# The order of wide and narrow products inside the FFN parts of a two-block transformer kernel

## What is computed

```python
def swiglu(x, w_gate, w_up, w_down):
    return (jax.nn.silu(x @ w_gate) * (x @ w_up)) @ w_down

h = h + 0.5 * swiglu(rms_norm(h, ffn1_norm[l]), ffn1_w_gate[l], ffn1_w_up[l], ffn1_w_down[l])   # FFNs 0 to 3
...
gu = h @ w_ffn_gu                                                                               # FFNs 4 and 5
ffn = (jax.nn.silu(gu[..., :D_FF_2]) * gu[..., D_FF_2:]) @ w_ffn_down
return x + rms_norm_2(ffn, n_post_ffn)
```

## Time and profile before

| | |
|---|---|
| median of 3 runs | 1903.11 us |
| the profiled execution's own time | 1903.32 us |
| its span | 1901.2 us |
| TensorE busy | 99% of the span |
| VectorE busy | 70% |
| ScalarE busy | 51% |
| GpSimd busy | 8% |
| DMA | 327.28 MB, 172 GB/s mean |

### The profile page before, as it was taken

The page is one execution under the profiler, slowest core; times in us unless marked ns, Lnnn a source line. Parts: engine busy times, 40 slices in busy tenths (PEclk is TensorE's granted clock), DMA queues, the critical chain, the costliest instruction groups (busy, mean ns, idle before and its releaser), DMA issues.

```text
span 1901.2 us, 26155 instructions
## 1 busy us (share of the span) xinstructions
PE 1889.3 (99%) x10937; PEld 1638.0 (86%) x10940; DVE 1339.7 (70%) x1485; ACT 967.6 (51%) x1216; POOL 161.4 (8%) x158
## 2 busy tenths in 40 slices
PE   9999999999999999999999999999999999999998
PEld 7888879988888888898888888888888888888887
DVE  7877687877687767868776555569765654568764
ACT  5444656544444446665444665455444665455442
POOL 0000522100000006121000200000000110000000
PEclk9999999999999999999999999999999999999999
DMA  7555542455555544334554443445545343445552
GB/s 284 210 183 179 188 150 104 163 190 181 189 199 179 187 184 177 133 112 177 191 188 169 160 175 133 163 170 189 188 172 187 136 172 136 159 176 182 183 175 113
DMA packets 47491, 327.28 MB, mean 172 GB/s; under 512 B 5520, under 2 KB 5520, under 8 KB 11536
## 3 DMA queue, kind: packets, MB, share of 16 engines
q1 hardware_dynamic: 46512, 323.25, 47.2%
q10 hardware_dynamic: 864, 2.38, 0.3%
HBM read 324.56 MB, written 1.05 MB: 171 GB/s over the span
## 4 chain that ended last, share of the span: by engine, by line
PE 98%; ACT 1%; issue 0%; DVE 0%; DMA 0%; POOL 0%; DVEq 0%; POOLq 0%; ACTq 0%
PE ps L537 34%; PE ps L541 18%; PE ps L525 10%; PE ps L527 10%; PE ps L526 10%; PE ps L531 2%; PE ps L833 2%; PE ps L788 1%; PE ps L790 1%; PE ps L789 1%; PE ps L799 1%; PE ps L532 1%; PE ps L822 1%; PE ps L554 1%; PE ps L709 1%; PE ps L849 0%
## 5 line engine op out<-in xcount | busy, mean ns | idle before, releaser
L331 ACT CAST w_hi<-raw 128x2048 fp32r<-128x2048 f32 (+4 forms) x314 | 580.5, 1850 | 585.0 <-PE ps L541 352.4
L338 DVE TENSOR_TENSOR w_lo<-raw,w_hi 128x2048 fp32r<-128x2048 f32 (+4 forms) x314 | 700.1, 2231 | 243.0 <-ACT w_hi L331 240.1
L537 PE MATMUL ps<-x_hl,w_hi 128*128 128x512 f32 x1968 | 494.2, 393 | 0.0
L537 PEld LDWEIGHTS ps<-x_hl,w_hi 128*128 128x128 f32 x1968 | 353.7, 189 | 63.6
L541 PEld LDWEIGHTS ps<-x_hl,w_lo 128*128 128x128 f32 x1968 | 268.5, 190 | 19.3
L541 PE MATMUL ps<-x_hl,w_lo 128*128 128x256 f32 x1968 | 274.4, 282 | 0.0
L525 PE MATMUL ps<-w_hi,x_hl 128*128 128x512 f32 (+3 forms) x672 | 262.5, 391 | 0.0
L527 PE MATMUL ps<-w_hi,x_hl 128*128 128x512 f32 (+3 forms) x672 | 254.2, 378 | 0.0
L526 PE MATMUL ps<-w_lo,x_hl 128*128 128x512 f32 (+3 forms) x672 | 253.6, 377 | 0.0
L1784 DVE TENSOR_REDUCE ffn_tmp<-ps 128x512 f32<-128x1024 f32 x132 | 161.2, 1222 | 103.0 <-PE ps L541 102.4
L537 PE MATMUL ps<-hid_hl,w_hi 128*128 128x512 f32 x836 | 211.1, 392 | 0.0
(11 more groups left out here) (288 smaller groups left out, 2203.6 us busy)
## 6 DMA issues: line engine op xcount, KB each, us to landing
raw<-in_parts SPq DMA_DIRECT2D x278, 1024.0 KB, 4.8
raw<-in_parts SPq DMA_DIRECT2D x20, 768.0 KB, 4.2
raw<-in_parts SPq DMA_DIRECT2D x4, 928.0 KB, 4.5
raw<-in_parts SPq DMA_DIRECT2D x4, 864.0 KB, 4.3
raw<-in_parts SPq DMA_DIRECT2D x6, 512.0 KB, 3.7
raw<-in_parts SPq DMA_DIRECT2D x4, 576.0 KB, 3.6
const<-in_const ACTq DMA_DIRECT2D x1, 1093.0 KB, 5.1
h<-in_x_t SPq DMA_DIRECT2D x1, 1024.0 KB, 7.6
```

The lines of the kernel that those rows point to most:

```text
L331: nc.scalar.copy(w_hi[:, i % RING, 0:n_of(i)], raw[:, i % RING, 0:n_of(i)]).then_inc(high_ready, 1)
L338: nc.vector.tensor_tensor(w_lo[:, s, 0:n], raw[:, s, 0:n], w_hi[:, s, 0:n].bitcast(F32), ALU.subtract).then_inc(low_ready, 1)
L537: nc.tensor.matmul(ps[:, bank, :], w_h(c), hl(c).rearrange("p x n -> p (x n)"), start=start and c == 0, stop=False, skip_group_check=True)
```

## The change

All but the first parts of an FFN now use the first order. Up parts behind the one with `to_rows` go chunk by chunk, wide and narrow in turn, banks alternating (`in_turn`), except FFN 5's four parts with `turn_h`. They wait for the whole part (`part_ready`) at their start. The parts with inserted products go through both banks wide (16 products), then the inserted products, then both banks narrow (`matmul_banks`); in FFNs 1, 3 and 5 the part with `to_rows` has narrow first and wide last (`narrow_first`), so that the parts in turn follow 16 wide products there, and 16 narrow ones in FFNs 0, 2 and 4. Down parts go in turn too, but for the last column block's third part, which keeps 8 wide and 8 narrow for each bank (and for FFN 4's last column block, which has three products of 256 columns for each chunk, as before). `chunk_done` is then told by the last but one pair of a block. No product, copy or transfer is added or removed.

```diff
+        def wide_run(bank, kc, w_h, hl, start, stop):
+            for c in range(kc):
+                m = nc.tensor.matmul(ps[:, bank, :], w_h(c), hl(c).rearrange("p x n -> p (x n)"), start=start and c == 0, stop=stop and c == kc - 1,
+                                     skip_group_check=True)
+            return m
...
+        def matmul_banks(bank, kc, hi, lo, hl, start, stop, narrow_first, low=None, between=None):
+            def wide(opens):
+                for f in range(2):
+                    m = wide_run(bank + f, kc, lambda c: hi[:, c, f * P:(f + 1) * P], hl, start and opens, stop and not opens)
+                return m
...
+            (narrow if narrow_first else wide)(True)
             if low is not None:
                 nc.tensor.wait_ge(low_ready, low)
...
+            if between is not None:
+                between()
+            return (wide if narrow_first else narrow)(False)
...
-                    by_half = p > 0 and i > 1
-                    if by_half:
+                    with_turn = s == LAST and p in (6, 9, 12, 15)
+                    in_turn = p == 0 or i == 1 or p > stats_at + 1 and not with_turn
+                    narrow_first = p == stats_at + 1 and FFN_BEFORE[s] % 2 == 1
+                    if i > 1 and (in_turn or narrow_first):
+                        part_ready(i)
+                    elif i > 1:
                         pe.wait_ge(high_ready, i + 1)
...
+                    if in_turn:
+                        for c, f in [(c, f) for c in range(KC) for f in range(2)]:
...
+                            m = matmul_pair(pair_banks(p) + f, hi[:, c, f * P:(f + 1) * P], lo[:, c, f * P:(f + 1) * P],
+                                            x_hl[:, c, :, :], c == 0, c == KC - 1)
...
+                        m = matmul_banks(pair_banks(p), KC, hi, lo, lambda c: x_hl[:, c, :, :], True, True, narrow_first,
+                                         None if narrow_first else i + 1, between)
...
+                        if q < KC // 2 - 1 or n < 2 and not post_norm:
+                            for k in range(kc):
+                                for c in range(2):
+                                    m = matmul_pair(down_bank(2 * q + c), hi[:, k, c * P:(c + 1) * P], lo[:, k, c * P:(c + 1) * P],
+                                                    hid_hl[:, k0 + k, :, :], k0 + k == 0, k0 + k == FF - 1)
+                                    if k0 + k == FF - 1 and c == 0:
+                                        m.then_inc(chunk_done, 1)
+                            m.then_inc(part_used, 1)
+                            continue
```

More of the change, by code:

```diff
@@ L532, in matmul_pair, with narrow_run, narrow @@
             return nc.tensor.matmul(ps[:, bank, 0:SEQ], w_l, hl[:, 0, :], start=False, stop=stop, skip_group_check=True)
-        def matmul_run(bank, kc, w_h, w_l, hl, start, stop, low=None):
+        def wide_run(bank, kc, w_h, hl, start, stop):
             for c in range(kc):
-                nc.tensor.matmul(ps[:, bank, :], w_h(c), hl(c).rearrange("p x n -> p (x n)"), start=start and c == 0, stop=False, skip_group_check=True)
+                m = nc.tensor.matmul(ps[:, bank, :], w_h(c), hl(c).rearrange("p x n -> p (x n)"), start=start and c == 0, stop=stop and c == kc - 1,
+                                     skip_group_check=True)
+            return m
+        def narrow_run(bank, kc, w_l, hl, start, stop):
+            for c in range(kc):
+                m = nc.tensor.matmul(ps[:, bank, 0:SEQ], w_l(c), hl(c)[:, 0, :], start=start and c == 0, stop=stop and c == kc - 1,
+                                     skip_group_check=True)
+            return m
[3 more added lines that the diff above has]
+                    m = wide_run(bank + f, kc, lambda c: hi[:, c, f * P:(f + 1) * P], hl, start and opens, stop and not opens)
+                return m
+            def narrow(opens):
+                for f in range(2):
+                    m = narrow_run(bank + f, kc, lambda c: lo[:, c, f * P:(f + 1) * P], hl, start and opens, stop and not opens)
+                return m
+            (narrow if narrow_first else wide)(True)
             if low is not None:
                 nc.tensor.wait_ge(low_ready, low)
-            for c in range(kc):
-                m = nc.tensor.matmul(ps[:, bank, 0:SEQ], w_l(c), hl(c)[:, 0, :], start=False, stop=stop and c == kc - 1, skip_group_check=True)
-            return m
+            if between is not None:
+                between()
+            return (wide if narrow_first else narrow)(False)
         @block.tensor
@@ L640, in ffn @@
                     i = i0 + p
-                    by_half = p > 0 and i > 1
-                    if by_half:
+                    with_turn = s == LAST and p in (6, 9, 12, 15)
[4 more added lines that the diff above has]
+                    elif i > 1:
                         pe.wait_ge(high_ready, i + 1)
-                    elif i > 1:
-                        part_ready(i)
                     if p >= 3:
@@ L648, in ffn, with between @@
                     hi, lo = view(w_hi, i), view(w_lo, i)
-                    order = [(c, f) for f in range(2) for c in range(KC)]
-                    if p == 0 or i == 1:
-                        order = [(c, f) for c in range(KC) for f in range(2)]
-                    else:
-                        order = []
-                        for f in range(2):
-                            if p == stats_at and f == 1:
+                    if in_turn:
+                        for c, f in [(c, f) for c in range(KC) for f in range(2)]:
+                            if i == 0 and c % 2 == 0 and f == 0:
+                                pe.wait_ge(*((first_lo, c // 2 + 1) if c < 6 else (low_ready, 1)))
+                            if i == 1 and c % 4 == 0 and f == 0:
+                                pe.wait_ge(*((first_lo, 4) if c == 0 else (low_ready, 2)))
+                            if p == 0 and f == 0:
+                                pe.wait_ge(xlo_ready, x0 + c + 1)
+                            m = matmul_pair(pair_banks(p) + f, hi[:, c, f * P:(f + 1) * P], lo[:, c, f * P:(f + 1) * P],
+                                            x_hl[:, c, :, :], c == 0, c == KC - 1)
+                    else:
+                        def between():
+                            if p == stats_at:
@@ L656, in ffn @@
                                 pe.wait_ge(const_in, 16)
                                 stats_sum(STATS_FFN)
-                            if p == stats_at + 1 and f == 1:
+                            if p == stats_at + 1:
                                 pe.wait_ge(root_ready, due("root_ready"))
                                 to_rows(STATS_FFN, rstd)
-                            if s == LAST and f == 1 and p in (6, 9, 12, 15):
+                            if with_turn:
                                 turn_h(p // 3 - 2)
-                            m = matmul_run(pair_banks(p) + f, KC, lambda c: hi[:, c, f * P:(f + 1) * P], lambda c: lo[:, c, f * P:(f + 1) * P],
-                                           lambda c: x_hl[:, c, :, :], True, True, i + 1 if by_half and f == 0 else None)
@@ L684, in ffn @@
                         hi, lo = view(w_hi, i), view(w_lo, i)
+                        if q == 0:
+                            pe.wait_ge(hidlo_ready, h0 + (k0 + kc) // 2)
+                        if q < KC // 2 - 1 or n < 2 and not post_norm:
[7 more added lines that the diff above has]
+                            continue
                         for c in range(2):
-                            if q == 0 and c == 0:
-                                pe.wait_ge(hidlo_ready, h0 + (k0 + kc) // 2)
-                            if post_norm and q == KC // 2 - 1:
+                            if post_norm:
                                 for k in range(kc):
@@ L692, in ffn @@
                             else:
-                                m = matmul_run(down_bank(2 * q + c), kc, lambda k: hi[:, k, c * P:(c + 1) * P], lambda k: lo[:, k, c * P:(c + 1) * P],
-                                               lambda k: hid_hl[:, k0 + k, :, :], k0 == 0, n == 2)
+                                wide_run(down_bank(2 * q + c), kc, lambda k: hi[:, k, c * P:(c + 1) * P], lambda k: hid_hl[:, k0 + k, :, :], False, False)
+                                m = narrow_run(down_bank(2 * q + c), kc, lambda k: lo[:, k, c * P:(c + 1) * P], lambda k: hid_hl[:, k0 + k, :, :], False, True)
                             if n == 2 and c == 0:
```

## The result

The changed kernel takes 1911.52 us (median of 5 runs, 1907.39 to 1913.96) where the kernel before takes 1903.11 in the same comparison: a ratio of 1.0043 [1.0032, 1.0053], so slower by over 0.2%. The forecast was 1912.8 in [1902.0, 1914.5]. What was not forecast as the likeliest is the spread: five runs of the kernel before lie within 0.54 us, the five of the changed one within 6.6.

What follows compares the result with a forecast made beforehand. TensorE, 99% busy, bounds the kernel through the spacing of its products' starts. Slow spacing +9.7, inserts -0.3, part 5's stops +0.2, FFN 5's root +0.1 make +9.7 on 1903.32: 1913.0, as median 1912.8 us, range 1902.0 to 1914.5.

Steps and rivals of the forecast that it cites:

- The spacing as the price: Distance between TensorE starts sets the time: in turn, slow 353.2 or fast 346.7 ns a pair, against 349.2 today.
- Entry from narrow and from wide products: Stretches in turn behind 16 narrow (FFNs 0, 2, 4) or 16 wide products (1, 3, 5): both taken as slow.
- The stop of part 5: FFNs 0 and 4: part 5's low split ends late, TensorE stops 0 to 0.3 us, twice: +0.2 us.
- I keep slow: Part 5's stop may change the spacing in FFNs 0 and 4; the slow spacing was assumed to stay behind it.
- the prediction's own sign: Sign of being wrong: parts of 5.55 us with narrow products of 274 to 280 ns in an FFN.
- all slow: Likeliest case: both entries and part 5's stops leave every FFN at the slow spacing, 1911.5 to 1914.5 us; chance 0.40.
- a stop makes FFN 0 or 4 fast: Rival: part 5's stop turns FFN 0 or 4 fast, 2.8 us less each: 1910 with one, 1907 with both; chance 0.17.
- The parts with inserts: 16 up parts with inserted products lose one narrow-to-wide switch, 20 ns each: -0.3 us, between -0.6 and 0.
- The down block: After a down column block, VectorE takes the second bank 1.3 us later; 1.6 us of cover stay: nothing.
- a late split: Rival: third down part after each column block late, each 0.1 us costing 1.5 us: above 1914.5; chance 0.03.
- The roots: POOL's root ahead of to_rows: in FFN 1 in time, nothing; in FFN 5 a stop of 0 to 0.3, put +0.1 us.
- Order changes nothing: Rival: a pair keeps its 349 ns in any order, only switches and stops count: 1903.1 us; chance 0.03.

Runs made afterwards that it cites:

- e1_covered: Changed kernel with parts 4 and 5 of FFNs 0 and 4 kept 16 wide, then 16 narrow; 1912.80 us, ratio 1.0049.
- e2_narrow: e1_covered with `narrow_first = False`, so all six FFNs enter the products in turn from 16 narrow ones; 1912.71 us.
- ten trials of FFN 3: Map of entries on the changed kernel: every second up part, behind wide products, begins with k more narrow products, k from 0 up; whole kernel 1906.78 us.
- e4_stops: e1_covered, but in FFNs 1 to 3 every second up part from 6 on waits until VectorE has emptied the part just before; 1953.87 us.
- e7_banks: Kernel before, with all up parts but the first ones going 16 wide, then 16 narrow, down parts as before; 1901.15 us, ratio 0.9988.
- e5_flip: e2_narrow, but the first part of every stretch in turn begins narrow, wide, narrow, wide; 1897.57 us, ratio 0.9969.
- e6_thirds: e5_flip with other numbers of flipped pairs: 1, 2, 3, 5, 4 in FFNs 0 to 4, and 8, 1, 2, 3, 5 in FFN 5; 1906.32 us.

## Why the prediction was right, step by step

**The spacing as the price: right.** e1_covered has no stop ahead of part 5, and 137 long and 19 short slow parts. By the prediction's prices that is 8.8 + 0.7 - 0.3 = +9.2 us; it measured 1912.80 - 1903.42 = +9.4.

**Entry from narrow and from wide products: right, both slow.** The profile and e2_narrow show it. The evidence put for the wide entry, the 278 ns of a single narrow product, was thin, and it did point the right way; a shortest duration of 274 isn't even the mark of the fast spacing, which also has 280 throughout. The wide entry is slow in all ten trials of FFN 3. The narrow entry, which looked the safer, is the one that two more wide products ahead, or two flipped pairs, make fast.

**The stop of part 5: right in place and size, its consequence not.** Stops of 0.1 us were found where 0 to 0.3 was put. The sentence "I keep slow" is the step that failed: in the three traces of this program FFN 0 is fast in all and FFN 4 in two. By the prediction's own sign, parts of 5.55 us with 274 to 280 ns, it was wrong for these two FFNs and right for the other four. The likeliest case, all slow at 1912.8, is therefore not the one that was profiled; *a stop makes FFN 0 or 4 fast*, "1910 with one, 1907 with both", is, and it measured 1910.48 and 1907.82. The profiled run by the terms of the sum: 1913.0 - 2 x 2.8 = 1907.4, measured 1907.39. Agreement to 0.01 us is luck: FFN 4 is worth 2.6 and not 2.8, and two small terms below are off by 0.1 to 0.2. The median lies between the cases, 1.3 us under the forecast, and the range holds since it was drawn across them; that the median came so near to a case that no trace of this program shows is in part luck too. A chance above 0.17 for this rival would have been the better reading: of the two stops in the rows one was followed by the fast spacing, and in e4_stops 10 of 24 were.

**The parts with inserts: -0.3 was too much.** The two such parts of FFN 2 and the start of the next part, before and then after (lines 537 are wide):

```profile
532.62 2.03 PE L537 MATMUL ps<-x_hl,w_hi 128*128 128x512 f32 x8
...
538.68 0.63 PE L537 MATMUL ps<-x_hl,w_hi 128*128 128x512 f32 x2
...
544.71 1.55 PE L537 MATMUL ps<-x_hl,w_hi 128*128 128x512 f32 x6
```

```profile
532.92 3.85 PE L537 MATMUL ps<-x_hl,w_hi 128*128 128x512 f32 x16
...
538.98 3.81 PE L537 MATMUL ps<-x_hl,w_hi 128*128 128x512 f32 x16
...
544.99 0.40 PE L531 MATMUL ps<-x_hl,w_hi 128*128 128x512 f32 x1
```

12.09 us became 12.07, not 12.05: the part with to_rows went from 6.03 to 6.01, the part with the sum stayed at 6.06. FFN 1's two parts stay at 12.09 (347.24 to 359.33 before, 345.64 to 357.73 after). By the starts in the two traces, the 15 such parts other than FFN 5's to_rows take 0.15 us less together, half of what was put. The switch price itself was right, as e7_banks shows; why some parts with an insert save it and others don't, no run shows. The prediction expected 6.02 us a part; in FFNs 1 and 2 it is 6.04 on average.

**The down block: right.** VectorE behind the first column block of FFN 0, to be set beside the earlier trace rows:

```profile
148.54 0.69 DVE L1893 TENSOR_REDUCE arena<-ps 128x256 f32<-128x512 f32 x1 [1.87 <-PE ps L532]
...
150.06 0.68 DVE L1893 TENSOR_REDUCE arena<-ps 128x256 f32<-128x512 f32 x1
...
154.41 4.49 DVE L338 TENSOR_TENSOR w_lo<-raw,w_hi 128x2048 fp32r<-128x2048 f32 x2 [1.35 <-ACT w_hi L331]
```

The second bank follows the first without a pause, 1.52 us behind it. The block's last pair ends 0.35 us behind the start of the first row, at 148.89, so the second bank is taken 1.17 us late, where 1.3 was put. (All of it is 1.2 us earlier than before, FFN 0 being fast.) The split waits for ScalarE's cast for 1.35 us, as it did before. In the list of what weight loads waited for (total us, times, longest), products in turn have one row for a low half:

```profile
PEld ps L531 <- DVE w_lo L338: 0.4, 2, 0.2
```

These are the two stops of part 5, in FFNs 0 and 4 (39.03 and 1313.91). No down part stands in it, so *a late split* is out; e1_covered's list has no such row.

**The roots: right in both.** GpSimd's roots and TensorE's `to_rows` (line 605 now) in FFNs 1 and 5, in FFN 5 its weight load:

```profile
350.30 2.69 POOL L2345 TENSOR_TENSOR stat<-stat,const 128x2 f32<-128x2 f32 x1 [6.32 <-DVE stat L1719]
...
353.62 0.60 PE L605 MATMUL ps<-const,stat 128*128 128x128 f32 x4
...
1729.74 2.67 POOL L2345 TENSOR_TENSOR stat<-stat,const 128x2 f32<-128x2 f32 x1 [19.72 <-DVE stat L1719]
...
1732.47 0.52 PEld L605 LDWEIGHTS ps<-const,stat 128*128 128x128 f32 x4 [0.19 <-POOL stat L2345]
```

FFN 1: the root is there 353.62 - 352.99 = 0.63 us early; 355.1 - 354.5 = 0.6 was worked out. FFN 5: the weight load was idle for 0.19 us until the root came at 1732.41, and began at 1732.47. The part takes 6.27 us where those with narrow first in FFNs 1 and 3 take 6.03, so this stop costs 0.2 us in this trace; in the two others of this program the part takes 6.11, under 0.1 more. 0 to 0.3 was the forecast, with +0.1 put.

**Order changes nothing: out.** The four spacings 346.7, 348 (5.566 / 16), 349.2 and 353.3 ns hold the same two products. The order matters by itself: e5_flip and e2_narrow differ in the order of four products at each entry and by 6.6 ns in the pairs that follow. The Trainium skill (TensorE: Matmul & The Clock Gate, section Back-to-back issue gap) gives the formula by columns alone, which the prediction used, for the gap of an isolated product, and says that in a stream of weight loads and products both set the spacing. So its 325 ns was no forecast for this stream, and these runs take 346.7 and more.

## What to carry to other kernels

When TensorE is full, measure the distance of starts over a long stretch for each order of products, and look whether the same order has more than one spacing; if it has, the entry is part of the design, and a trial of a few entries inside one kernel, set apart by runs of another order, maps them in one execution. A spread of several us in a kernel whose neighbour repeats within 0.5 is a sign that something short (here a wait of 0.1 us) chooses between two lasting states: cover it first, then choose the state by the order. Long runs of one size are the safe choice where no such choice can be made (e7_banks, -2.1 us with nothing to hit or miss).

## What the runs showed of the hardware that was not expected

- The same two products in turn have a slow spacing that repeats over three pairs (starts 350, 361 and 349 ns apart in the trace's own ns, e1_covered) and a fast one (347 throughout, or 350 and 343 in turn, e4_stops). Either is kept over some 460 pairs without a stop.
- Behind narrow products and without a stop the order of the first products decides, the same way in every FFN tried: two or three more wide products ahead (FFNs 1 and 2) or two flipped pairs (all six) give 346.7 ns, and flipped pairs count by threes (2, 5, 8 fast). That a flip moves the meeting of two wide products by one step of a cycle of three fits this and was what e6_thirds was built on; what in the engine has three steps, no run shows. Behind wide products none of the ten entries tried was fast.
- In e4_stops a stop ended a fast stretch each time (9 of 9) and a slow one two times in three (10 of 15). It needn't be long: the 0.1 us at part 5 does what 34.8 / 24 = 1.45 us does in e4_stops. In the three traces of the changed kernel it ended five of six slow stretches, and in FFN 5 of e5_flip and e6_thirds a stop at the same place ended a fast one.
- The best order, e5_flip, runs at the sum of what a product costs in a settled run of its own kind (226.7 ns wide, 120 ns narrow, from the starts in e7_banks' runs of sixteen): in turn, with the right entry, the switches cost nothing.
